# Neighborhood attention: K and V projected in halves that reach into the task loop, and an output projection issued in quarters

## The chip, the cores and the metric

The program runs on one core of one Trainium2 chip. The metric is the device time of one execution in microseconds (us), lower is better; the median of several executions is given. The engines are named as in the profile: PE is TensorE, DVE is VectorE, ACT is ScalarE, POOL is GpSimd, SP is SyncE, which issues nearly all of the DMAs.

## What is computed

The reference is two transformer layers and a third block over 256 tokens of width 1024, all in float32. Only the neighborhood attention of the second layer is touched by the change. Its input `h` is 256 x 1024; 16 heads of 64; the tokens are a grid of 4 rows and 64 columns, and a query at column c sees the 16 columns around it in all 4 rows.

```python
def _neighborhood_attention(h, w_in, w_out, rpb):
    q, k, v = jnp.split(h @ w_in, 3, axis=-1)          # w_in is 1024 x 3072
    ...
    def row_step(r):
        ...
        sc = jnp.einsum('bqhd,brqjhd->bhqrj', q_row, k_win).astype(jnp.float32) * scale
        sc = sc + bias.astype(jnp.float32)[None]
        p = jax.nn.softmax(sc.reshape(b, nh, GRID_W, kh * kw), axis=-1)
        ...
        return jnp.einsum('bhqrj,brqjhd->bqhd', p, v_win)
    o = lax.map(row_step, jnp.arange(rows))
    return o @ w_out                                    # w_out is 1024 x 1024
```

It is followed by a norm, a residual add and a feed-forward layer, called `f3` in the kernel.

## The kernel before

**Weights come in units.** A unit is 128 partitions x 2 x 512 numbers, numbered through the whole program, in a ring of RING = 6 slots. SP loads it into `raw` (`load`, L258; the two DMAs are L263), ACT rounds it into `whi` (`hi`, L265 to L272), DVE forms the rest `wlo` (`lo`, L274 to L280), and PE uses it in 12 matmuls of 512 columns, three for each pair of row block and token half (`mm3`, L282 to L289; `held_rows` and `first_chunk` do the same in another order). `hi` of unit n waits until PE has used unit n - 6; the load of unit n waits for `lo` of unit n - 6. Each engine has one instruction stream in a fixed order, and SP too: a load that waits holds up every DMA behind it.

**The projection.** `w_in` is taken in six chunks of 512 output columns, four units each: e = 0, 1 are Q, 2, 3 are K, 4, 5 are V (`chunk_pe`, L775). When a chunk is done, ACT copies token half 0 and DVE token half 1 out of PSUM into `qkv` (`evac_act` L795, `evac_dve` L802, counted in `s_qa` and `s_qv`). After chunk 4 `qk_turn` (L845) transposes Q in 16 PE instructions (L857), ACT and DVE copy it into `qB` (L1087, L1093), then, after one unit of chunk 5, it transposes K, which ACT and DVE copy into `kT` by column (L1102, L1107, four copies each, counted in `s_kta` and `s_ktv`).

**The task loop.** There are 16 tasks: a pair of heads p = 0..7 and a token half t. Task i goes through `scores(i)` on PE (L1134), bias and row maximum on DVE (L1223, L1227), two exponentials on ACT (L1208), the division on DVE (L1232, L1233), `turn(i)` on PE (L1146), a copy on ACT (L1203) and `pv(i)` on PE (L1158). PE issues per iteration: `scores(i)`, then `between(i)`, `turn(i-2)`, `pv(i-3)`. After every second task ACT and DVE split a finished head pair into `xhi` (L1184) and `xlo` (L1191), the left operand of the output projection. ACT and DVE call `between(i)` at the head of iteration i: there stand the `hi` and `lo` of coming units and the copy of chunk 5 out of PSUM.

**What PE does between the tasks** before: units 1 to 3 of chunk 5 (i = 0 to 3), and units 0 and 1 of the output projection `out1` in halves of six matmuls (i = 10, 11, 14, 15). Units 2 and 3 follow the loop; unit 4 is the first of `end_rows` (L817), then come units 5 to 7 in `held_rows` (L376 to L378).

**V by column window.** `pv` reads V from `vwin`, in the order of the column windows. `na_values_sp` (L1109, DMAs at L1117) fills it with SBUF to SBUF DMAs, 16 for each half of V, issued by SP: the first 16 after unit 6 of `out1` (wait: chunk 4 is in `qkv`), the second 16 after the load of unit j = 1 of `f3` (wait: chunk 5 is in `qkv`). `pv(0)` waits for the first 16, `pv(8)` for the second 16. Behind the second 16 SP goes on with the loads of `f3`.

Of the kernel before, what the change touches and what calls it, by code (L numbers as in the profile page):

```python
# [59 lines left out]
def build(nc, x, norm_g, ffn1_wg, ffn1_wu, ffn1_wd, ffn2_wg, ffn2_wu, ffn2_wd, diff_w_in, diff_w_out,  # L60
# [5 lines left out]
    with ctx:  # L66
# [74 lines left out]
        exw = ex[:, :, 0, :].rearrange("p b (q k) -> p b q k", q=2)  # L141
# [68 lines left out]
        s_vw = sem("window_values_landed")  # L210
# [551 lines left out]
        def proj_sp(sp, n0, w, cols=(0, 1), late=None):  # L762
            part_sp(sp, n0, w, cols)
            for j in range(UP, KT):
                down_unit(sp, n0 + j, 0, w, j * P)
                if j == 6 and late is not None:
                    late()


        def chunk_bank(e, t, m=0):  # L770
            if m == 1 and e == 5:
                return Y + 2 * t
            return (Y if e == 0 else Z + 2 * (e % 2)) + t
# [42 lines left out]

        def end_rows(pe, n0, r, nr):  # L817
# [11 lines left out]
        NEX = 3  # L829

# [11 lines left out]
        def turn_bank(kind, bk):  # L842
            return (Z + 2, Z + 3, Y + 1, Y + 3)[bk] if kind == "na" else Y + bk

        def qk_turn(pe, m, kind, which):  # L845

            for bk in range(4):
                if which == 1 and kind != "na":
                    pe.wait_ge(s_qta, 2 * m + bk + 1)
                if which == 1 and kind == "na":  # L850
                    pe.wait_ge(s_qte, 2 * bk + 2)
                    pe.wait_ge(s_qtd, 2 * bk + 2)
                for p in (2 * bk, 2 * bk + 1):
                    c0 = qk_cols(kind, p)[which]
                    for t in range(NT):
                        o = ps[:, turn_bank(kind, bk), (p % 2) * S + t * P:(p % 2) * S + (t + 1) * P]
                        ins = nc.tensor.transpose(o, qkv[:, t, c0:c0 + P], ident)  # L857
                ins.then_inc(s_qt, 1)
# [236 lines left out]
        def by_column(rows, bk):  # L1095
            return (kT[rows, 2 * bk:2 * bk + 2, :].rearrange("p a (c g) -> p a g c", g=GR),
                    ps[rows, turn_bank("na", bk)].rearrange("p (a g c) -> p a g c", a=2, g=GR))

        def na_k_act(act):
            for bk in range(4):  # L1100
# [3 lines left out]
        def na_k_dve(dve):  # L1104
            for bk in range(4):
# [12 lines left out]

        def na_pe(pe, between):
            b = NTASK  # L1120
            pe.wait_ge(s_kz, 4)
            pe.wait_ge(s_qa, 6 + 5)
            pe.wait_ge(s_qv, 6 + 5)
# [14 lines left out]
            def turn(i):  # L1138
                if i == 0:
                    pe.wait_ge(s_ktv, 8)  # L1140
                    pe.wait_ge(s_kta, 8)
                pe.wait_ge(s_a, b + i + 1)
                if i >= 2:
                    pe.wait_ge(s_ate, b + i - 1)
                for q in range(2):
                    ins = nc.tensor.transpose(ps[:, Y + 1 + 2 * (i % 2), q * P:(q + 1) * P], exw[:, i % NEX, q], ident)  # L1146
# [31 lines left out]
        def na_out_act(act, n0, p):  # L1178
            act.wait_ge(s_pv, NTASK + 2 * p + 2)
            if p == 0:  # L1180
                act.wait_ge(s_used, used(n0 + 23))
# [12 lines left out]
        def na_act(act, n0, between):  # L1194
            b = NTASK
            for i in range(NTASK + 2):
                between(i)
                if i >= 2:
                    j = i - 2
# [4 lines left out]
                if i < NTASK:  # L1204
                    p, t = TASKS[i]
                    act.wait_ge(s_mx, b + i + 1)
                    for q in range(2):
                        nc.scalar.activation(exw[:, i % NEX, q], exw[:, i % NEX, q], ACT.Exp, bias=nmx[:, i % 2, q:q + 1],  # L1208
                                             accum_out=rs[:, t, 2 * p + q:2 * p + q + 1]).then_inc(s_ex, 1)
                if i >= 5 and i % 2 == 1:  # L1210
                    na_out_act(act, n0, (i - 5) // 2)
            na_out_act(act, n0, 7)

        def na_dve(dve, steps, between):
            b = NTASK
            for i in range(NTASK + 1):
                between(i)
                if i < NTASK:
                    p, t = TASKS[i]
                    dve.wait_ge(s_sc, b + i + 1)  # L1220
                    if i >= NEX:
                        dve.wait_ge(s_at, b + i - 2)
                    steps.done(nc.vector.tensor_tensor(exw[:, i % NEX], ps[:, Z + i % 2, 0:2 * P].rearrange("p (q k) -> p q k", q=2),  # L1223
# [3 lines left out]
                    nc.vector.tensor_reduce(nmx[:, i % 2], exw[:, i % NEX], AX_X, ALU.max, negate=True).then_inc(s_mx, 1)  # L1227
                if i >= 1:
# [4 lines left out]
                    nc.vector.tensor_tensor(exw[:, j % NEX], exw[:, j % NEX],  # L1233
                                            ri[:, t, 2 * p:2 * p + 2].unsqueeze(2).broadcast_to([P, 2, P]), ALU.mult).then_inc(s_a, 1)
                if i >= 6 and i % 2 == 0:
                    na_out_dve(dve, (i - 6) // 2)
# [150 lines left out]
        def _(sp):  # L1387
# [14 lines left out]
            chunk_sp(sp, n["qkv1"], na_w_in[0], [512 * c for c in range(6)])  # L1402
# [93 lines left out]
        def _(act):  # L1496
# [22 lines left out]

            def qkv_act(m, n0, r):  # L1520
# [5 lines left out]
                if m == 1:  # L1526
                    na_q_act(act)
                    tops_act(act, n0 + UP * 5, range(1))
                    na_k_act(act)

                    def na_between(i):
                        if i == 5:
                            evac_act(act, 1, n0, 5, r, IN_ORDER)
                        if i in (1, 2, 5):
                            hi(act, n0 + UP * 5 + RING + (i + 2) // 2)
                        if i in (12, 16):
                            hi(act, n["out1"] + RING + i // 4 - 3)
                    return na_between
# [27 lines left out]
            na_act(act, n["qkv1"], qkv_act(1, n["qkv1"], 4))  # L1566
# [72 lines left out]
        def _(dve):  # L1639
# [18 lines left out]

            def qkv_dve(m, n0, r, rotate):
# [10 lines left out]
                if m == 1:  # L1670
                    na_q_dve(dve)
                    tops_dve(dve, n0 + UP * 5, range(1))
                    na_k_dve(dve)

                    def na_between(i):
                        if i == 5:
                            evac_dve(dve, 1, n0, 5, r, IN_ORDER)
                        if i in (2, 3, 6):
                            lo(dve, n0 + UP * 5 + RING + (i + 1) // 2)
                        if i in (13, 17):  # L1680
                            lo(dve, n["out1"] + RING + i // 4 - 3)
                    return na_between
# [36 lines left out]
            between = qkv_dve(1, n["qkv1"], 4, False)  # L1719
# [126 lines left out]
        def _(pe):  # L1846
# [13 lines left out]
            def qkv_pe(m, n0, r, kind):  # L1860
# [3 lines left out]
                if kind == "diff":  # L1864
                    pe.wait_ge(s_qr, 1)
                    pe.wait_ge(s_cst2, 16)
# [17 lines left out]
                def na_between(i):  # L1884
                    if i in (0, 1):
                        chunk_pe(pe, 1, n0, 5, range(i + 1, i + 2))
                    if i in (2, 3):
                        last_chunk_half(pe, n0 + UP * 5 + 3, 3, i - 2, Y, Y + 2)
# [3 lines left out]
                    if i in (10, 11, 14, 15):  # L1892
                        part_unit(pe, no, 6, i // 14, 0, (Y, Y + 2), (i % 2,))
                return na_between if m == 1 else between
# [16 lines left out]
            na_pe(pe, qkv_pe(1, n["qkv1"], 5, "na"))  # L1911
# [127 lines left out]
```

## Time and profile before

| | us |
|---|---|
| median of 3 executions | 1411.9 (1410.58 to 1412.84) |
| the profiled execution | 1412.99 |
| its span, first to last instruction | 1411.2 |
| PE busy in the span | 1387.1 |
| DVE busy | 874.5 |
| ACT busy | 752.6 |

All times in the rows are microseconds from the start of the span of that one execution. Matmuls are pipelined: a row's duration (0.39 for 512 columns) is longer than the distance to the next start (0.227), so costs on PE are taken from start to start. In the view by stretches "PEclk" is the granted TensorE clock as a share of full speed.

### The profile page before, as it was taken

Reading aid. Unit: us, or ns where it says so; the run is one execution under the profiler, and the core shown is the slowest. Engines: PE = TensorE matmul, PEld = TensorE weight load, DVE = VectorE, ACT = ScalarE, POOL = GpSimd, SP = SyncE. Lnnn points to the kernel's source line nnn. Section 1 sums busy time; section 2 is a strip of 40 time slices with the busy share of each in tenths; the row PEclk is TensorE's granted clock in tenths of the full one; section 3 lists DMA queues with packets and bytes.
Section 4 is the critical chain, followed back from the end, with each engine's and each line's share of the span. In section 5 each row is a group of like instructions: output and inputs, shape, how many; then the busy total and the mean of one; then the engine's idle time right before and its main releaser. Section 6 shows DMA issues by size and latency. Waiting matters only on the chain.

```text
span 1411.2 us, 20415 instructions
## 1 busy us (share of the span) xinstructions
PE 1387.1 (98%) x6556; PEld 1146.9 (81%) x6556; DVE 874.5 (62%) x1231; ACT 752.6 (53%) x1292; POOL 108.6 (8%) x168
## 2 busy tenths in 40 slices
PE   8999999999999999999999899999999999999999
PEld 6888878878888888888887788888888898788887
DVE  5555566777555566555666865555667876575564
ACT  6444465566444465444555765444555565565553
POOL 2322210011001000000010000000013000000000
PEclk9999999999999999999999999999999999999999
DMA  8966747315655647556555337656575523555551
GB/s 273 253 207 195 223 129 255 111 46 180 207 181 191 203 136 228 184 188 192 180 196 185 99 118 225 191 186 201 178 224 164 173 67 111 185 184 181 182 180 50
DMA packets 192565, 248.43 MB, mean 176 GB/s; under 512 B 17127, under 2 KB 130035, under 8 KB 192384
## 3 DMA queue, kind: packets, MB, share of 16 engines
q1 hardware_dynamic: 189472, 243.40, 54.8%
q0 software_dynamic: 2928, 4.31, 1.3%
q8 instruction: 30, 0.49, 0.1%
q14 instruction: 23, 0.19, 0.0%
q10 hardware_dynamic: 112, 0.05, 0.0%
HBM read 244.40 MB, written 1.18 MB: 174 GB/s over the span
## 4 chain that ended last, share of the span: by engine, by line
PE 94%; DVE 3%; ACT 2%; issue 1%; DMA 0%; ACTq 0%; DVEq 0%
PE ps L287 25%; PE ps L289 25%; PE ps L288 25%; PE ps L317 2%; PE ps L324 2%; PE ps L314 2%; PE ps L672 1%; PE ps L904 1%; PE ps L376 1%; PE ps L339 1%; PE ps L378 1%; PE ps L377 1%; ACT whi L272 1%; DVE wlo L280 1%; PE ps L1274 1%
## 5 line engine op out<-in xcount | busy, mean ns | idle before, releaser
L280 DVE TENSOR_TENSOR wlo<-raw,whi 128x1024 fp32r<-128x1024 f32 x450 | 546.6, 1226 | 351.5 <-ACT whi L272 350.9
L272 ACT CAST whi<-raw 128x1024 fp32r<-128x1024 f32 x450 | 468.9, 1051 | 324.4 <-PE ps L289 314.3
L287 PE MATMUL ps<-whi,xhi 128*128 128x512 f32 x1196 | 470.9, 394 | 0.3 <-DVE xlo L482 0.3
L289 PE MATMUL ps<-whi,xlo 128*128 128x512 f32 x1196 | 466.8, 390 | 0.0
L288 PE MATMUL ps<-wlo,xhi 128*128 128x512 f32 x1196 | 466.3, 390 | 0.0
L289 PEld LDWEIGHTS ps<-whi,xlo 128*128 128x128 f32 x1196 | 224.9, 188 | 47.3
L287 PEld LDWEIGHTS ps<-whi,xhi 128*128 128x128 f32 x1196 | 225.3, 188 | 46.3 <-issue 0.5
L288 PEld LDWEIGHTS ps<-wlo,xhi 128*128 128x128 f32 x1196 | 225.4, 188 | 45.9
L287 PE MATMUL ps<-whi,thi 128*128 128x512 f32 x384 | 153.8, 401 | 0.0
L289 PE MATMUL ps<-whi,tlo 128*128 128x512 f32 x384 | 150.2, 391 | 0.0
L288 PE MATMUL ps<-wlo,thi 128*128 128x512 f32 x384 | 149.7, 390 | 0.0
L694 ACT CAST thi<-ps 128x256 fp32r<-128x256 f32 x80 | 29.4, 373 | 106.5 <-PE ps L672 57.8
L289 PEld LDWEIGHTS ps<-whi,tlo 128*128 128x128 f32 x384 | 72.1, 188 | 15.6
L288 PEld LDWEIGHTS ps<-wlo,thi 128*128 128x128 f32 x384 | 72.3, 188 | 13.9
L287 PEld LDWEIGHTS ps<-whi,thi 128*128 128x128 f32 x384 | 72.2, 188 | 13.6
L685 ACT ACTIVATE qkv<-ps,rx 128x256 f32<-128x256 f32 x88 | 36.9, 471 | 67.8 <-PE ps L289 66.4
L720 DVE SCALAR_TENSOR_TENSOR qkv<-ps,rx,qkv 128x256 f32<-128x256 f32 x88 | 38.6, 480 | 39.2 <-ACT qkv L685 39.2
L729 DVE TENSOR_TENSOR tlo<-ps,thi 128x256 fp32r<-128x256 f32 x80 | 33.6, 424 | 41.3 <-ACT thi L694 41.3
L557 POOL TENSOR_SCALAR ry<-ssy 128x1 f32<-128x1 f32 x12 | 3.6, 300 | 592.2 <-ACT sqa L542 592.2
L317 PE MATMUL ps<-wlo,xhi 128*128 128x512 f32 x128 | 40.2, 395 | 1.7 <-DVE wlo L280 1.7
L314 PE MATMUL ps<-whi,xhi 128*128 128x512 f32 x128 | 41.1, 402 | 0.6 <-ACT whi L272 0.6
L1449 POOL DMA_DIRECT2D aux<-rpb_scratch x64 | 35.3, 559 | 75.6 <-PE ps L672 71.2
(209 smaller groups left out, 1239.0 us busy)
## 6 DMA issues: line engine op xcount, KB each, us to landing
raw<-in_ffn_wg_dram SPq DMA_DIRECT2D x176, 256.0 KB, 2.9
raw<-in_ffn_wu_dram SPq DMA_DIRECT2D x176, 256.0 KB, 3.1
raw<-in_ffn_wd_dram SPq DMA_DIRECT2D x176, 256.0 KB, 3.0
raw<-in_w_ffn_up_dram SPq DMA_DIRECT2D x88, 256.0 KB, 3.6
raw<-in_w_in_dram SPq DMA_DIRECT2D x80, 256.0 KB, 3.4
raw<-in_diff_w_in_dram SPq DMA_DIRECT2D x48, 256.0 KB, 3.2
raw<-in_na_w_in_dram SPq DMA_DIRECT2D x48, 256.0 KB, 3.2
raw<-in_w_ffn_down_dram SPq DMA_DIRECT2D x44, 256.0 KB, 3.2
```

What stands on the lines that cost most here:

```text
L272: nc.scalar.copy(whi[:, s], raw[:, s]).then_inc(s_hi, 1)
L280: nc.vector.tensor_tensor(wlo[:, s], raw[:, s], whi[:, s].bitcast(F32), ALU.subtract).then_inc(s_lo, 1)
L287: nc.tensor.matmul(outs[t], ahi[:, c], whi[:, s, i], start=start, stop=False)
L288: nc.tensor.matmul(outs[t], ahi[:, c], wlo[:, s, i], start=False, stop=False)
L289: last = nc.tensor.matmul(outs[t], alo[:, c], whi[:, s, i], start=False, stop=stop)
L314: nc.tensor.matmul(o, xhi[:, 2 * j + i, c], whi[:, s, i], start=j == 0 and i == 0, stop=False)
L317: nc.tensor.matmul(o, xhi[:, 2 * j + i, c], wlo[:, s, i], start=False, stop=False)
L685: nc.scalar.activation(silu[:, t], ps[:, base + t, 0:FC], ACT.Silu, scale=rx[:, t:t + 1]).then_inc(s_si, 1)
L694: nc.scalar.copy(thi[:, j], ps[:, Z + 2 + j, 0:S]).then_inc(s_hth, 1)
L720: nc.vector.scalar_tensor_tensor(out=hs[:, t], in0=ps[:, base + t, FC:2 * FC], scalar=rx[:, t:t + 1], in1=silu[:, t], op0=ALU.mult, op1=AL ...
L729: nc.vector.tensor_tensor(tlo[:, j], ps[:, Z + 2 + j, 0:S], thi[:, j].bitcast(F32), ALU.subtract).then_inc(s_htl, 1)
L1449: pool.dma_start(nab[cc::16, :, w], src).then_inc(s_nab, 16)
```

## The change

Q is transposed after chunk 2 and no longer after chunk 4. The order of the chunks becomes Q, Q, K first half, V first half, K second half, V second half (`NA_ORDER`). The first half of K is transposed after chunk 3; chunk 4 (K second half) has its unit 0 ahead of the loop and units 1 to 3 in iterations 0 to 2; its transposes stand in iteration 4, and in iteration 5 PE waits for all K copies. Chunk 5 runs in iterations 5 to 8, one unit each, and units 0 and 1 of `out1` in iterations 10 to 17 in quarters of three matmuls. `turn` lags `scores` by three iterations and `pv` by four; the buffers `exw` for probabilities go from 3 to 6. ACT and DVE get the same moves in their `between`. The DMAs into `vwin` are issued after unit 3 of `out1` (first half) and after unit j = 3 of `f3` (second half), and each group of 8 has a semaphore of its own. The number of matmuls, DMAs and copies is the same.

```diff
-        exw = ex[:, :, 0, :].rearrange("p b (q k) -> p b q k", q=2)
+        exw = ex[:].rearrange("p b c (q k) -> p (b c) q k", q=2)
...
         def proj_sp(sp, n0, w, cols=(0, 1), late=None):
             part_sp(sp, n0, w, cols)
+            if late is not None:
+                late()
             for j in range(UP, KT):
                 down_unit(sp, n0 + j, 0, w, j * P)
-                if j == 6 and late is not None:
-                    late()
...
+        def part_quarter(pe, n0, r, u, at):
+            pe.wait_ge(s_lo, RING + n0 + u + 1)
+            j, s, i, t = u % 2, slot(n0 + u), at // 2, at % 2
+            pe.wait_ge(s_xl, XB[r] + 2 * j + 2)
+            k, c, o = 2 * j + i, slice(t * P, (t + 1) * P), ps[:, Y + 2 * t]
+            nc.tensor.matmul(o, xhi[:, k, c], whi[:, s, i], start=k == 0, stop=False)
+            nc.tensor.matmul(o, xhi[:, k, c], wlo[:, s, i], start=False, stop=False)
+            last = nc.tensor.matmul(o, xlo[:, k, c], whi[:, s, i], start=False, stop=False)
...
+        NA_ORDER = [0, 1, 2, 4, 3, 5]
...
         def na_values_sp(sp, half):
-            sp.wait_ge(s_qa, 6 + 5 + half)
-            sp.wait_ge(s_qv, 6 + 5 + half)
+            sp.wait_ge(s_qa, 6 + 4 + 2 * half)
+            sp.wait_ge(s_qv, 6 + 4 + 2 * half)
...
-                    sp.dma_start(vwin[r::GR, w, c], qkv[p0:p0 + 32, r // 2, 2 * D + c.start:2 * D + c.stop]).then_inc(s_vw, 16)
+                    sp.dma_start(vwin[r::GR, w, c], qkv[p0:p0 + 32, r // 2, 2 * D + c.start:2 * D + c.stop]).then_inc(s_vw[2 * half + w // 2], 16)
...
-                if i in (0, 8):
-                    pe.wait_ge(s_vw, 16 * 16 * (i // 8 + 1))
+                if i % 8 < 2:
+                    pe.wait_ge(s_vw[i // 8 * 2 + i % 8], 16 * 8)
...
-            for i in range(NTASK + 3):
+            for i in range(NTASK + 4):
                 if i < NTASK:
                     scores(i)
                 between(i)
-                if 2 <= i < NTASK + 2:
-                    turn(i - 2)
-                if i >= 3:
-                    pv(i - 3)
+                if 3 <= i < NTASK + 3:
+                    turn(i - 3)
+                if i >= 4:
+                    pv(i - 4)
...
-            ffn_sp(sp, n["f3"], *ffn_w[3], 5, lambda j: na_values_sp(sp, 1) if j == 1 else None)
+            ffn_sp(sp, n["f3"], *ffn_w[3], 5, lambda j: na_values_sp(sp, 1) if j == 3 else None)
...
+            def na_qkv_dve(n0, r):
+                for e in range(4):
+                    tops_dve(dve, n0 + UP * e)
+                    evac_dve(dve, 1, n0, e, r, NA_ORDER)
+                    if e == 2:
+                        na_q_dve(dve)
+                na_k_dve(dve, range(2))
+                lo(dve, n0 + UP * 4 + RING)
+                def between(i):
+                    if i == 3:
+                        evac_dve(dve, 1, n0, 4, r, NA_ORDER)
+                    if i == 5:
+                        na_k_dve(dve, range(2, 4))
+                    if i == 9:
+                        evac_dve(dve, 1, n0, 5, r, NA_ORDER)
+                    if i in (2, 3, 4):
+                        lo(dve, n0 + UP * 4 + RING + i - 1)
+                    if i in (7, 8, 9, 10):
+                        lo(dve, n0 + UP * 5 + RING + i - 7)
+                    if i in (15, 17):
+                        lo(dve, n["out1"] + RING + i // 17)
+                return between
...
+            def na_qkv_pe(n0, r):
+                first_chunk(pe, n0, r)
+                for e in (1, 2):
+                    chunk_pe(pe, 1, n0, e, range(UP))
+                ...
+                qk_turn(pe, 1, "na", 0)
+                chunk_pe(pe, 1, n0, 3, range(UP))
+                ...
+                qk_turn(pe, 1, "na", 1, range(2))
+                chunk_pe(pe, 1, n0, 4, range(1))
+                def between(i):
+                    if i in (0, 1, 2):
+                        chunk_pe(pe, 1, n0, 4, range(i + 1, i + 2))
+                    if i == 4:
+                        pe.wait_ge(s_qa, 6 + 5)
+                        pe.wait_ge(s_qv, 6 + 5)
+                        qk_turn(pe, 1, "na", 1, range(2, 4))
+                    if i == 5:
+                        pe.wait_ge(s_kta, 8)
+                        pe.wait_ge(s_ktv, 8)
+                    if i in (5, 6, 7, 8):
+                        chunk_pe(pe, 1, n0, 5, range(i - 5, i - 4))
+                    if i == 10:
+                        pe.wait_ge(s_qa, 12)
+                        pe.wait_ge(s_qv, 12)
+                    if 10 <= i < 18:
+                        part_quarter(pe, n0 + 24, 6, (i - 10) // 4, (i - 10) % 4)
+                return between
```

ACT has the mirror of the DVE part (`na_qkv_act`): the same copies at i = 3, 5 and 9, the `hi` of units at i = 1, 2, 3, then 6 to 9, then 14 and 18.

## Rows read from the trace of the kernel before

**Rows 1.** Page: busy time, share of the span and instructions of each engine.
```profile
PE 1387.1 (98%) x6556; PEld 1146.9 (81%) x6556; DVE 874.5 (62%) x1231; ACT 752.6 (53%) x1292; POOL 108.6 (8%) x168
```

**Rows 2.** Stretches: busy PE, PEld, DVE, ACT, POOL; PEclk; DMA share; GB/s.
```profile
768.00:771.40 3.40, 3.40 (x10) 2.62 (x9) 2.30 (x4) 2.28 (x6) 0.00 (x0) 0.51 0.41 102
...
788.40:792.00 3.60, 3.44 (x17) 3.44 (x18) 3.05 (x11) 2.72 (x13) 0.00 (x0) 0.53 0.42 110
...
808.80:812.40 3.60, 3.55 (x13) 3.16 (x14) 2.45 (x5) 1.63 (x5) 0.00 (x0) 0.53 0.39 109
...
758.40:819.60 61.20, 54.02 (x302) 45.53 (x300) 45.96 (x103) 41.54 (x120) 0.00 (x0) 0.92 0.39 112
```

**Rows 3.** Waits of PE, 756 to 826: waiter, releaser, total, times, longest.
```profile
PE ps L1146 <- DVE ex L1233: 3.2, 6, 1.2
...
PE ps L1134 <- DVE kT L1107: 1.8, 1, 1.8
```

**Rows 4.** PE in time order: start, duration, line, count; idle before in brackets.
```profile
736.72 0.39 PE L287 MATMUL ps<-whi,xhi 128*128 128x512 f32 x1
...
758.48 1.91 PE L857 MATMUL ps<-cst,qkv 128*128 128x128 f32 x16
760.15 0.48 PE L287 MATMUL ps<-whi,xhi 128*128 128x512 f32 x1
...
767.14 0.68 PE L1134 MATMUL ps<-kT,qo 128*128 128x128 f32 x4 [1.82 <-DVE kT L1107]
...
772.01 0.61 PE L1134 MATMUL ps<-kT,qo 128*128 128x128 f32 x4
...
775.23 0.60 PE L1134 MATMUL ps<-kT,qo 128*128 128x128 f32 x4
...
779.77 0.61 PE L1134 MATMUL ps<-kT,qo 128*128 128x128 f32 x4
780.22 0.38 PE L1146 MATMUL ps<-cst,ex 128*128 128x128 f32 x2
780.44 0.61 PE L1158 MATMUL ps<-aT,aux 128*128 128x128 f32 x4
780.88 0.61 PE L1134 MATMUL ps<-kT,qo 128*128 128x128 f32 x4
...
796.54 0.61 PE L1158 MATMUL ps<-aT,aux 128*128 128x128 f32 x4
...
819.66 0.39 PE L376 MATMUL ps<-whi,xhi 128*128 128x512 f32 x1
```

**Rows 5.** DVE in time order: Q and K copies, a task, `lo`, copy-out, split.
```profile
761.73 2.82 DVE L1093 TENSOR_SCALAR qo<-ps 64x256 f32<-64x256 f32 x8
...
765.84 3.79 DVE L1107 COPY kT<-ps 64x512 f32<-64x512 f32 x4
...
772.66 0.42 DVE L1223 TENSOR_TENSOR ex<-ps,aux 128x256 f32<-128x256 f32 x1 [2.32 <-PE ps L1134]
...
773.99 1.22 DVE L280 TENSOR_TENSOR wlo<-raw,whi 128x1024 fp32r<-128x1024 f32 x1
...
781.74 0.75 DVE L802 TENSOR_SCALAR qkv<-ps,rx 128x512 f32<-128x512 f32 x1
...
786.21 0.85 DVE L1191 TENSOR_TENSOR xlo<-ps,xhi 64x256 fp32r<-64x256 f32 x2
```

**Rows 6.** ACT in time order: the four K copies.
```profile
764.30 3.81 ACT L1102 COPY kT<-ps 64x512 f32<-64x512 f32 x4
```

**Rows 7.** SP's queue in time order: start, time of the issues, line, count.
```profile
761.78 10.10 SPq L1117 DMA_DIRECT2D aux<-qkv  x16
...
782.81 10.23 SPq L1117 DMA_DIRECT2D aux<-qkv  x16
793.08 0.58 SPq L263 DMA_DIRECT2D raw<-in_ffn_wg_dram  x1
```

**Rows 8.** The same 32 DMAs by line: time from issue to landing.
```profile
DMA to landing us min/median/max: 2.0/2.1/2.2
```

More of the change, by code:

```diff
@@ L209, in build @@
         s_ilv = sem("rpb_interleaved")
-        s_vw = sem("window_values_landed")
+        s_vw = [sem(f"window_values_landed{i}") for i in range(4)]
         s_qtd = sem("qT_second_head_ready")
@@ L840, in keys, with turn_bank, qk_turn @@
             return t + 1 if kind == "b2" else NT
[L842 to L847, printed above, removed]
+        def turn_bank(kind, bk, which=0):
+            return (Y + 1, Y + 3, Y, Y + 2)[bk] if kind == "na" and which == 1 else Y + bk
+        def qk_turn(pe, m, kind, which, banks=range(4)):
+            for bk in banks:
                 if which == 1 and kind != "na":
                     pe.wait_ge(s_qta, 2 * m + bk + 1)
-                if which == 1 and kind == "na":
-                    pe.wait_ge(s_qte, 2 * bk + 2)
-                    pe.wait_ge(s_qtd, 2 * bk + 2)
                 for p in (2 * bk, 2 * bk + 1):
@@ L855, in qk_turn @@
                     for t in range(NT):
-                        o = ps[:, turn_bank(kind, bk), (p % 2) * S + t * P:(p % 2) * S + (t + 1) * P]
+                        o = ps[:, turn_bank(kind, bk, which), (p % 2) * S + t * P:(p % 2) * S + (t + 1) * P]
                         ins = nc.tensor.transpose(o, qkv[:, t, c0:c0 + P], ident)
@@ L1096, in by_column, with na_k_act, na_k_dve @@
             return (kT[rows, 2 * bk:2 * bk + 2, :].rearrange("p a (c g) -> p a g c", g=GR),
-                    ps[rows, turn_bank("na", bk)].rearrange("p (a g c) -> p a g c", a=2, g=GR))
-        def na_k_act(act):
-            for bk in range(4):
+                    ps[rows, turn_bank("na", bk, 1)].rearrange("p (a g c) -> p a g c", a=2, g=GR))
+        def na_k_act(act, banks):
+            for bk in banks:
                 act.wait_ge(s_qt, 8 + 4 + bk + 1)
                 nc.scalar.copy(*by_column(slice(HD, P), bk)).then_inc(s_kta, 1)
-        def na_k_dve(dve):
-            for bk in range(4):
+        def na_k_dve(dve, banks):
+            for bk in banks:
                 dve.wait_ge(s_qt, 8 + 4 + bk + 1)
@@ L1195, in na_act @@
             b = NTASK
-            for i in range(NTASK + 2):
+            for i in range(NTASK + 3):
                 between(i)
-                if i >= 2:
-                    j = i - 2
+                if i >= 3:
+                    j = i - 3
                     act.wait_ge(s_at, b + j + 1)
@@ L1207, in na_act @@
                     for q in range(2):
-                        nc.scalar.activation(exw[:, i % NEX, q], exw[:, i % NEX, q], ACT.Exp, bias=nmx[:, i % 2, q:q + 1],
+                        nc.scalar.activation(exw[:, i % NEXW, q], exw[:, i % NEXW, q], ACT.Exp, bias=nmx[:, i % 2, q:q + 1],
                                              accum_out=rs[:, t, 2 * p + q:2 * p + q + 1]).then_inc(s_ex, 1)
-                if i >= 5 and i % 2 == 1:
-                    na_out_act(act, n0, (i - 5) // 2)
+                if i >= 6 and i % 2 == 0:
+                    na_out_act(act, n0, (i - 6) // 2)
             na_out_act(act, n0, 7)
@@ L1232, in na_dve @@
                     steps.done(nc.vector.reciprocal(ri[:, t, 2 * p:2 * p + 2], rs[:, t, 2 * p:2 * p + 2]))
-                    nc.vector.tensor_tensor(exw[:, j % NEX], exw[:, j % NEX],
+                    nc.vector.tensor_tensor(exw[:, j % NEXW], exw[:, j % NEXW],
                                             ri[:, t, 2 * p:2 * p + 2].unsqueeze(2).broadcast_to([P, 2, P]), ALU.mult).then_inc(s_a, 1)
-                if i >= 6 and i % 2 == 0:
-                    na_out_dve(dve, (i - 6) // 2)
+                if i >= 7 and i % 2 == 1:
+                    na_out_dve(dve, (i - 7) // 2)
+            na_out_dve(dve, 5)
             between(NTASK + 1)
@@ L1518, in _, with na_qkv_act @@
             post_act(act, 0, 1, n["f0"] + 65, 0.5, 1, gainA(0, 2), 1)
+            def na_qkv_act(n0, r):
+                for e in range(4):
+                    tops_act(act, n0 + UP * e)
+                    evac_act(act, 1, n0, e, r, NA_ORDER)
+                    if e == 2:
+                        na_q_act(act)
+                na_k_act(act, range(2))
+                hi(act, n0 + UP * 4 + RING)
+                def between(i):
+                    if i == 3:
+                        evac_act(act, 1, n0, 4, r, NA_ORDER)
+                    if i == 5:
+                        na_k_act(act, range(2, 4))
+                    if i == 9:
+                        evac_act(act, 1, n0, 5, r, NA_ORDER)
+                    if i in (1, 2, 3):
+                        hi(act, n0 + UP * 4 + RING + i)
+                    if i in (6, 7, 8, 9):
+                        hi(act, n0 + UP * 5 + RING + i - 6)
+                    if i in (14, 18):
+                        hi(act, n["out1"] + RING + i // 18)
+                return between
             def qkv_act(m, n0, r):
@@ L1718, in _ @@
             post_dve(dve, steps, 3, n["f2"] + 65, 5, gainA(1, 2))
-            between = qkv_dve(1, n["qkv1"], 4, False)
+            between = na_qkv_dve(n["qkv1"], 4)
             dve.wait_ge(s_nar, NAP)
@@ L1863, in qkv_pe @@
                     chunk_pe(pe, m, n0, e, range(UP))
[L1864 to L1866 removed]
+                pe.wait_ge(s_qr, 1)
+                pe.wait_ge(s_cst2, 16)
                 pe.wait_ge(s_qa, 6 * m + 4)
@@ L1891, in na_between @@
                         pe.wait_ge(s_qv, 12)
-                    if i in (10, 11, 14, 15):
-                        part_unit(pe, no, 6, i // 14, 0, (Y, Y + 2), (i % 2,))
-                return na_between if m == 1 else between
+                    if 10 <= i < 18:
+                        part_quarter(pe, n0 + 24, 6, (i - 10) // 4, (i - 10) % 4)
+                return between
             def last_chunk_half(pe, n0, j, i, b0, b1):
```

73 lines of the change are left out of this document (29 added, 44 removed).

## The prediction

> **What bounds the kernel now.** The page comes first: PE is busy 98% of the span [rows 1], so the time is PE's work plus the few places where PE waits or runs slowly. In the stretches the reader looks for busy PE and granted clock together. From the end of chunk 4 (758.4) to the start of the last three projection units (819.6) PE is busy 54.0 of 61.2 us, and three spells of some 3.5 us inside it have a granted clock of 0.51 to 0.53, which is the 1.2 GHz level [rows 2]. The other stretches of the trace lose little of either kind, so this is the only place where the change can win much. The waits say who is late there: `turn` waits for DVE's division, 3.2 us in 6 places, and the first `scores` waits 1.8 us for DVE's K copies [rows 3]. DVE is busy 46.0 of the 61.2 us, ACT 41.5 [rows 2]: between the filled iterations DVE sets the pace, not PE.
>
> **Prices on PE**, start to start. 96 matmuls of 512 columns lie between 736.72 and 758.48, 0.227 each, so a unit is 2.72 and a chunk 10.9 [rows 4]. Q's 16 transposes take 1.67, half of them 0.84. An iteration with `scores` and one unit takes 3.22 (772.01 to 775.23). In a bare one `scores` is 0.45, `turn` 0.22, `pv` 0.44, together 1.11. The first `scores` and its unit took 4.87 instead of 3.22, so a slow spell costs 1.65 [rows 4].
>
> **Prices elsewhere.** DVE: a task 1.33, of which about 0.9 until the maximum; `lo` 1.2; copy-out 0.75; split 0.85; a K copy 0.95 [rows 5]. ACT's K copy is 0.95 too [rows 6]. SP: 16 value DMAs of 64 KB take 10.2 us to issue, 0.64 each, and each lands 2.1 after its issue [rows 7, 8]. One DMA of a load is 0.58, a unit has two; I take 1.0 for both [rows 7].
>
> **What is neutral.** PE gets the same matmuls and transposes. Quarters instead of halves cost some 0.09 more for each change of operand type (four more changes, 0.4, counted below). More `exw` buffers and four semaphores cost no instruction. The extra lag of one iteration gives `turn` one more iteration for the division; what it removes is the 3.2 us of rows 3, and what is late next is DVE's total work or a wait listed below.
>
> **The walk, before the loop.** The Q turn starts at 736.72, after chunk 2, and the V chunk ends at 736.72 + 1.67 + 10.97 = 749.4. Half of K's turn and unit 0 of chunk 4 end at 753.0. DVE is free 3.25 after PE ends a chunk (758.48 to 761.73), and the first `scores` came 1.30 after DVE's first K copy began (765.84 to 767.14) [rows 4, 5]: 749.4 + 4.55 = 753.9. So PE idles 0.9 here instead of 1.8.
>
> **Iterations 0 to 8.** Three iterations with a unit: 753.9 + 3 x 3.22 = 763.6. In iteration 3 DVE stands at the copy-out of chunk 4 (763.8 to 764.6), then `lo` to 765.8, then adds bias and maximum for task 3, to 766.6. PE does `scores(3)`, `turn(0)`, `scores(4)`, K's second turn (from 764.7 to 765.5), `turn(1)`, `pv(0)` and `scores(5)`, to 767.0. Then it meets the added wait for all K copies. On DVE these stand behind the rest of task 3 (0.45), a `lo` (1.2) and task 4 (1.33): 769.6, and two copies end at 771.5. PE goes on at 771.7, after some **4.7 us idle**. Queued behind that wait on PE are unit 0 of chunk 5, `turn(2)` and `pv(1)`; ACT's copy and DVE's later tasks wait for those, but have time. The restart is charged with one slow spell, 1.65, as after the 1.8 us wait of before. 771.7 + 2.8 + 0.67 + 1.65 = 776.8. Iterations 6 and 7 take 3.89 each, iteration 8 to the end of its unit 3.22. Chunk 5 is done at **787.9**, called E.
>
> **The second half of V.** What decides here is a queue. SP can issue the second 16 value DMAs only behind the load of `f3` unit 3, and that load waits for `lo` of the unit six before it, which is now DVE's `between(10)`. After E, DVE does: copy-out (E + 1.0), `lo` (2.2), task 9 (3.5), a split (4.4), `lo` (5.6). SP issues the load until 6.6, then the values: the 8th is issued at 11.1 and lands at 13.2, the 16th is issued at 16.2 and lands at **E + 18.3**. Before, the second 16 were issued from 782.81, 13.7 us ahead of `pv(8)` at 796.54, of which issue and landing need 12.3 [rows 4, 7, 8]: there was little slack. Now PE comes to `pv(8)` at about E + 9.0: it ends iteration 8 and does iteration 9 and `scores(10)` by E + 2.2, waits to 4.4 for the split that quarter 0 needs, ends iteration 10 at 5.8 (quarter 0.68, `turn` and `pv` 0.66), iteration 11 at 7.6, and stands before `pv(8)` of iteration 12 after another 1.4. `pv(8)` waits from 9.0 to 13.2, `pv(9)` after one more iteration from 15.0 to 18.3. Nothing else stands ready on PE, since its order is fixed. Loads of `f3` units 4 onward queue behind the values on SP, but PE wants them only after the whole norm and the first chunk, over 20 us later: no cost.
>
> **The end.** From `pv(9)`: 0.44, two iterations at 1.85, two without `scores` at 1.4, `turn(15)` and `pv(14)` 0.67, a wait of 0.8 for ACT (a `hi` stands before its last copy) and 0.44: 8.8. Then three units of out1, 8.2. E + 18.3 + 8.8 + 8.2 = 823.2, against 819.66 before: +3.6. A slow spell after the wait of `pv(9)` adds 1.65. **Sum: +5.3 us.** The profiled execution took 1412.99, its span 1411.2; it would become 1418.3. It lies 1.1 above the median of the runs, so for the median I say 1411.9 + 5.3 = 1417.2. The clock spells of the old stretch (three, about 5) are in its 61.2; the new walk has two in it.
>
> **The row against the page.** Rows 7 and 8 make the issue the slow part: a value DMA costs SP 0.64, 16 of them 10.2, while one lands in 2.1. The Trainium skill, DMA: Bandwidth & Descriptors, section "Issuing engines are not separate DMA queues", says that the time a sequencer needs to start a DMA is usually small beside the DMA itself. By it the 16 would land almost together; the case is priced below without the page. By that rule, the trace doesn't agree for these DMAs of 32 partitions.
>
> **Bounds of what before doesn't show.** The wait for K copies in the loop: at least 1.8, as before with the copies right behind the turn, at most 4.7 as walked; I take 4.7, since the order on DVE is fixed. Slow spells: none to four times 1.65; I take two, after the waits longer than the 1.8 that brought one before.
>
> **Rivals.**
> 1. *The values land in time* (issue cheap or overlapped, so that all 16 land about 2.1 after E + 6.6 = E + 8.7, before `pv(8)` at 9.0). Then both waits at `pv` go: E + 9.0 + 0.44 + 1.4 + 8.8 + 8.2 = E + 27.8 = 815.7, with no second spell: 4.0 before the old 819.7, **faster**, 1407.9. For it: the same DMAs held nobody before. Against it: SP's rows show 0.64 for each in both groups. It decides if the first 8 land before E + 9. Chance 0.15.
> 2. *K copies cost PE only half* (idle 2.4 and no slow spell after it), values late as forecast: 5.3 - 2.3 - 1.65 = +1.4, 1413.3, within 0.2%. For it: if DVE ran ahead of the walk in iterations 3 and 4. Chance 0.13.
> 3. *Slow spells also at the first `scores` and at the end* (before had one at each): +3.3 more, +8.6, 1420.5. For it: short waits of 0.4 to 1.0 at the end of before brought one. Chance 0.12.
> 4. *The forecast*, 1414.5 to 1420 by itself: chance 0.58. The remaining 0.02 goes to a gain of another kind, as a second cover of waits by the longer lag.
>
> **How the numbers follow.** Forecast 1417.2. The range reaches from just above rival 1, 1409.0, to rival 3 with a us for the walk, 1421.5; outside it lie about 0.15 and 0.05. 0.2% is 2.8 us, about what a measurement of this kernel can tell from no change. Slower by more: forecast and rival 3, 0.70. Within: rival 2 and a little more, 0.14. Faster: rival 1, 0.16.
>
> **What would show it.** In PE's order of time after: `scores(0)` near 753.9; a gap of 4 to 5 us before the first matmul of chunk 5 whose releaser is a K copy; E near 788; two gaps, at `pv(8)` and `pv(9)`, with a DMA into `aux` as releaser, and SP's 16 value issues beginning 6 to 7 us after E. The start of `held_rows` near 825. If `pv` shows no DMA gap the queue argument is wrong, and the result is rival 1. If the K gap is under 2.5, it is rival 2. If the division still holds `turn`, the extra lag didn't do what it says.

## The result

| | before | after |
|---|---|---|
| median, us | 1412.02 (1410.58 to 1412.84, 5 runs) | 1419.05 (1418.12 to 1421.4, 5 runs) |
| ratio to before | | 1.0053, 95% interval 1.0042 to 1.0064 |
| profiled execution, us | 1412.99 | 1421.4 |
| end of chunk 2 to the start of `held_rows`, us | 82.94 | 88.17 |

The change makes the kernel slower by 7.0 us. 1417.2 was forecast, with a range of 1409.0 to 1421.5.

The page of after: PE has 2.1 us more busy time than in [rows 1], DVE and ACT the same within 0.3, and the span is 8.4 us longer. So nearly all of it is waiting, not work. Of the 8.4 us, 5.2 lie between the end of chunk 2 and `held_rows`; the other 3.2 passed in the first 26 us of this one execution, before anything that the change touches.

```profile
span 1419.6 us, 20424 instructions
PE 1389.2 (98%) x6556; PEld 1149.0 (81%) x6556; DVE 874.7 (62%) x1231; ACT 752.4 (53%) x1292; POOL 107.9 (8%) x168
PE 94%; DVE 3%; ACT 1%; issue 1%; SPq 1%; DMA 1%; ACTq 0%; DVEq 0%
```

The last line is the chain that ended last: SP's queue and DMA have a share in it now. The waits of PE between 730 and 840 (waiter, releaser, total, times, longest):

```profile
PE ps L287 <- ACT kT L1114: 4.6, 1, 4.6
PE ps L1168 <- DMA aux<-qkv: 3.3, 1, 3.3
PE ps L1168 <- issue: 2.3, 1, 2.3
PE ps L824 <- DVE xlo L1201: 1.9, 1, 1.9
PE ps L1144 <- issue: 0.6, 1, 0.6
PE ps L1168 <- ACT aT L1213: 0.5, 1, 0.5
```

In sum these are 13.2 us. Before, PE waited 6.9 us in the same place: the 3.2 and 1.8 of [rows 3], and

```profile
PE ps L1158 <- ACT aT L1203: 1.9, 3, 1.0
```

Against [rows 3], `turn` no longer waits for the division, and the first `scores` waits 0.6 instead of 1.8. In their place PE waits 4.6 for the K copies ahead of chunk 5 (L287), 1.9 for a split ahead of quarter 0 (L824), and 2.3 and 3.3 at `pv(8)` and `pv(9)` (L1168). These are the new waits in order of time, with PE's landmarks around them:

```profile
739.88 1.91 PE L869 MATMUL ps<-cst,qkv 128*128 128x128 f32 x16
...
756.94 0.68 PE L1144 MATMUL ps<-kT,qo 128*128 128x128 f32 x4 [0.60 <-issue]
...
774.82 0.50 PE L287 MATMUL ps<-whi,xhi 128*128 128x512 f32 x1 [4.63 <-ACT kT L1114]
...
790.86 0.38 PE L1156 MATMUL ps<-cst,ex 128*128 128x128 f32 x2
...
795.17 0.47 PE L824 MATMUL ps<-whi,xhi 128*128 128x512 f32 x1 [1.93 <-DVE xlo L1201]
...
803.82 0.68 PE L1168 MATMUL ps<-aT,aux 128*128 128x128 f32 x4 [2.27 <-issue]
...
809.13 0.99 PE L1168 MATMUL ps<-aT,aux 128*128 128x128 f32 x4 [3.27 <-DMA aux<-qkv]
...
819.32 0.71 PE L1168 MATMUL ps<-aT,aux 128*128 128x128 f32 x4 [0.51 <-ACT aT L1213]
...
828.05 0.39 PE L376 MATMUL ps<-whi,xhi 128*128 128x512 f32 x1
```

The `turn` at 790.86 is the first instruction behind chunk 5: the point called E. What held the K copies is in the streams of DVE and ACT. DVE's copies (772.33) stand behind the `lo` at 769.88 and task 4, ACT's (772.82) behind the exponentials of task 4:

```profile
769.88 1.22 DVE L280 TENSOR_TENSOR wlo<-raw,whi 128x1024 fp32r<-128x1024 f32 x1
771.01 0.41 DVE L1233 TENSOR_TENSOR ex<-ps,aux 128x256 f32<-128x256 f32 x1
...
772.33 1.93 DVE L1119 COPY kT<-ps 64x512 f32<-64x512 f32 x2
...
772.82 1.95 ACT L1114 COPY kT<-ps 64x512 f32<-64x512 f32 x2
```

What held `pv` is in SP's stream. DVE ends the `lo` that starts at 795.05 at 796.28, SP issues the last load of `f3`'s first four at 796.31, and only then the 16 value DMAs:

```profile
795.05 1.23 DVE L280 TENSOR_TENSOR wlo<-raw,whi 128x1024 fp32r<-128x1024 f32 x1
...
796.31 0.37 SPq L263 DMA_DIRECT2D raw<-in_ffn_wg_dram  x1
796.72 0.47 SPq L263 DMA_DIRECT2D raw<-in_ffn_wu_dram  x1
797.29 10.23 SPq L1129 DMA_DIRECT2D aux<-qkv  x16
```

At `pv(8)` the profile names no releaser ("issue"). The eighth of the 16 is issued some 4.5 us after the first, at 801.8, and with 2.1 to land that gives 803.9, where `pv(8)` goes on at 803.82; k_gap_filled below names the DMA there.

Stretches, with the columns of [rows 2]: three slow spells again (stretches at half the clock), behind the K gap, behind the wait of quarter 0, and behind `pv(9)`.

```profile
774.60:778.00 3.40, 3.18 (x8) 2.55 (x9) 0.87 (x3) 0.17 (x1) 0.00 (x0) 0.59 0.02 6
...
795.60:799.10 3.50, 3.50 (x15) 3.08 (x14) 2.58 (x7) 2.03 (x9) 0.00 (x0) 0.51 0.54 162
...
809.10:812.70 3.60, 3.57 (x15) 3.20 (x16) 1.62 (x5) 0.00 (x0) 0.00 (x0) 0.53 0.02 5
```

### The profile page after: what moved, and what is told of

The parts are those of the page before. It is cut to its first block, busy times and chain, and to the rows that moved or that the text cites. A ratio compares the mean times of both kernels' runs of the same rounds, so it can differ in the third digit from the quotient of the medians.

```text
span 1419.6 us, 20424 instructions
## 1 busy us (share of the span) xinstructions
PE 1389.2 (98%) x6556; PEld 1149.0 (81%) x6556; DVE 874.7 (62%) x1231; ACT 752.4 (53%) x1292; POOL 107.9 (8%) x168
## 4 chain that ended last, share of the span: by engine, by line
PE 94%; DVE 3%; ACT 1%; issue 1%; SPq 1%; DMA 1%; ACTq 0%; DVEq 0%
PE ps L287 25%; PE ps L289 25%; PE ps L288 25%; PE ps L324 2%; PE ps L317 2%; PE ps L314 2%; PE ps L672 1%; PE ps L916 1%; PE ps L376 1%; PE ps L378 1%; PE ps L377 1%; PE ps L339 1%; DVE wlo L280 1%; PE ps L1285 1%; PE ps L952 1%
## 5 line engine op out<-in xcount | busy, mean ns | idle before, releaser
L287 PE MATMUL ps<-whi,xhi 128*128 128x512 f32 x1188 | 467.2, 393 | 4.9 <-ACT kT L1114 4.6
L287 PEld LDWEIGHTS ps<-whi,xhi 128*128 128x128 f32 x1188 | 223.5, 188 | 50.6 <-ACT kT L1114 4.8
L287 PE MATMUL ps<-whi,thi 128*128 128x512 f32 x384 | 153.8, 401 | 0.0
L287 PEld LDWEIGHTS ps<-whi,thi 128*128 128x128 f32 x384 | 72.2, 188 | 13.6
```

Of the source, the lines that this page charges most:

```text
L287: nc.tensor.matmul(outs[t], ahi[:, c], whi[:, s, i], start=start, stop=False)
```

## The experiments

"Stage" is the time from the end of chunk 2 to the first matmul of `held_rows`, read in one profiled execution. For kernels in the order of before, the end of chunk 2 is taken 21.76 us ahead of the end of chunk 4, as in [rows 4]. Medians of before in the three groups of runs were 1412.78, 1412.48 and 1411.86.

The mean granted clock of every one of these runs is on record too, and it tells how much of a run was spent in slow spells: one spell of 3.4 us at half the clock takes 0.0012 off the mean. The profiled executions bear this out (three spells 0.996, one 0.999, none 1.000). The 69 runs of before, by their mean clock:

| mean clock | 1.000 | 0.999 | 0.998 | 0.997 | 0.996 | 0.995 |
|---|---|---|---|---|---|---|
| runs | 8 | 8 | 18 | 7 | 19 | 9 |
| mean time, us | 1409.1 | 1410.4 | 1411.8 | 1412.0 | 1413.1 | 1414.3 |

"At equal clock" below means a comparison with this table.

### values_j1 and values_pool: who issues the second half of V, and behind what

```diff
-            ffn_sp(sp, n["f3"], *ffn_w[3], 5, lambda j: na_values_sp(sp, 1) if j == 3 else None)
+            ffn_sp(sp, n["f3"], *ffn_w[3], 5, lambda j: na_values_sp(sp, 1) if j == 1 else None)
```

> The kernel after, with one edit: the second 16 value DMAs stand behind f3's load j = 1 again, not j = 3. Theory (SP's queue sets the waits at pv(8) and pv(9)): they are issued from E + 1.0, right behind the copy-out of chunk 5, not from E + 6.5; the 8th lands at E + 7.6, before PE needs it, and the 16th at E + 12.7 instead of E + 18.3. The wait at pv(8) goes, about 2 us remain at pv(9), the stage from Q's turn to held_rows shrinks by 5.6 us, by 7.2 if the slow spell behind pv(9) goes too: median 1412 to 1413.5. Rival (DVE's work would hold PE there anyway): less than 2 us of gain, the gaps move to turn and scores.

In values_pool the call stands in POOL's stream, behind its memsets of `qB`:

```diff
-            ffn_sp(sp, n["f3"], *ffn_w[3], 5, lambda j: na_values_sp(sp, 1) if j == 3 else None)
+            ffn_sp(sp, n["f3"], *ffn_w[3], 5, None)
...
+            na_values_sp(pool, 1)
```

> The kernel after, with the second 16 value DMAs issued by POOL instead of SP. POOL has nothing else to do then and waits only for chunk 5's copy-out. Theory: issue from E + 1.0 at 0.56 each (POOL's rate for its small DMAs), the 8th lands near E + 7.3, the 16th near E + 12; SP's loads don't move. Same gain as with j = 1, 6 to 8 us. Rival (the DMAs themselves are slow, not their place in SP's queue): they land as late, measured from their first issue, as before, and PE's waits stay above 5 us in sum.

Measured: values_j1 1415.84 (ratio to before 1.0019, 1.0009 to 1.0029), stage 84.67; values_pool 1413.59 (1.0009, 0.9998 to 1.002), stage 82.43. PE and then SP of values_j1 in time order, E at 788.96:

```profile
788.96 0.38 PE L1156 MATMUL ps<-cst,ex 128*128 128x128 f32 x2
...
803.81 1.19 PE L1168 MATMUL ps<-aT,aux 128*128 128x128 f32 x4 [2.35 <-DMA aux<-qkv]
```

```profile
791.90 10.23 SPq L1129 DMA_DIRECT2D aux<-qkv  x16
```

POOL and then PE of values_pool, E at 788.41:

```profile
791.61 8.61 POOL L1129 DMA_DIRECT2D aux<-qkv  x16 [74.20 <-ACT qkv L795]
```

```profile
801.88 0.68 PE L1168 MATMUL ps<-aT,aux 128*128 128x128 f32 x4 [0.98 <-DMA aux<-qkv]
```

The place in the queue is the cause: the same DMAs, issued sooner, take away the 2.3 us at `pv(8)` and leave 2.35 (SP) and 0.98 (POOL) of the 3.27 at `pv(9)`. Both gains missed the expectation, which was 5.6 us or more: values_j1 gained 3.2 us in the median and 3.5 in the stage, values_pool 5.5 and 5.7. In values_j1 the issue began at E + 2.9, not E + 1.0: chunk 5's copy-out on ACT stands behind a copy, two exponentials and a split, and POOL names it as its releaser. So `pv(9)` went on at E + 14.9 instead of E + 18.3, which is 3.4 of the 3.5 us of the stage. The slow spell behind it came in after and in values_j1 alike. On POOL the 16 issues were also 1.6 us shorter, `pv(9)` went on at E + 13.5, and there was no spell behind it.

### k_copies_early: the K copies ahead of a `lo` and of task 4

```diff
-                    if i == 5:
+                    if i == 4:
                         na_k_dve(dve, range(2, 4))
```

and the same on ACT.

> The kernel after, with the K copies of banks 2 and 3 on ACT and DVE in between(4) instead of between(5), so ahead of one lo and of task 4's add, maximum and division. Theory (the 4.6 us gap before chunk 5's unit 0 is DVE's and ACT's order): the gap shrinks to about 2.1 us, E and everything behind it come 2.5 us sooner, 4.1 if the slow spell after the gap goes too: median 1415 to 1416.5. Rival (DVE is the bound over the stage): the work that was overtaken comes back before pv(8), gain under 1 us.

Measured: 1414.92 (1.002, 1.0009 to 1.0032), stage 84.25, 3.9 less than after. The gap is 2.19 (PE in time order), and there is no slow spell behind it (the stretch, columns as in [rows 2]):

```profile
769.04 0.50 PE L287 MATMUL ps<-whi,xhi 128*128 128x512 f32 x1 [2.19 <-ACT kT L1114]
```

```profile
769.00:773.00 4.00, 3.96 (x23) 3.37 (x23) 3.02 (x9) 1.89 (x8) 0.00 (x0) 1.00 0.55 188
```

2.4 us of gap and 1.6 of spell make up the 3.9 by which the stage is shorter, near the 4.1 expected at best. The waits behind it are the same as in after within 0.1 us, so nothing of the gain comes back, and DVE isn't the bound there.

### k_gap_filled: idle work in the gap

```diff
                     if i == 5:
+                        keep_warm(pe, 19, ps[:, Z + 3, 0:P])
                         pe.wait_ge(s_kta, 8)
```

> The kernel after, with 19 matmuls of the identity by itself (results unused, into a PSUM bank that is free) on PE right before the wait for the K copies, some 4.2 us of work in a gap of 4.6. Theory (the slow spell behind the gap comes from PE's idleness): the granted clock behind the gap stays at the full level, and the stage shrinks by the spell's 1.6 us: median 1417.4. Rival (the spell has another cause): PEclk is near 0.5 for some 3.4 us there as before, no gain.

Measured: 1418.34 (1.0044, 1.0029 to 1.0059), stage 87.24, 0.9 less than after. The clock behind the gap stays full, and E comes 49.45 us after chunk 2 instead of 50.98. The stretch behind the gap, and PE at `pv(8)`:

```profile
771.80:775.80 4.00, 3.98 (x23) 3.42 (x23) 0.70 (x3) 0.68 (x4) 0.00 (x0) 1.00 0.01 4
```

```profile
799.88 1.20 PE L1168 MATMUL ps<-aT,aux 128*128 128x128 f32 x4 [4.52 <-DMA aux<-qkv]
```

So in this execution filling the gap kept the spell away. Of the 1.5 us, 0.6 were lost again: one of SP's issues took 1.2 us instead of 0.6, the 16 took 10.86 instead of 10.23, and `pv(9)` went on at E + 18.9 instead of E + 18.3.

```profile
792.71 10.86 SPq L1129 DMA_DIRECT2D aux<-qkv  x16
```

The median gained 0.7 us, less than the 1.6 expected. The idle work does not always help: the mean clock was 0.998 in two of the eight runs, 0.996 in three and 0.995 in three, against 0.994 to 0.996 in the nine of after. At equal clock it is as slow as after.

### after_again and before_again: the same kernels once more

> The kernel after, unchanged. Its first profile has the stage from Q's turn to held_rows at 88.2 us, 5.2 more than before, but Q's turn itself 3.2 us later than before, from the first 26 us of the program, which the change doesn't touch. Theory: the stage is 88.2 us again within 0.3, and the start of Q's turn moves by some us from execution to execution without regard to the change; median 1418 to 1419.5. Rival (the change also slows the start): Q's turn at 739.5 to 740 again.

> The kernel before, unchanged, to see its own stage again. Its first profile had three slow spells in the stage and took 82.9 us from the end of chunk 2 to held_rows; before_j3, the same order of work plus a wait of 2.0 us, had none and took 81.3. Theory: the waits of PE are the same in every execution (6.9 us), and the number of slow spells is not: 0 to 3, each 1.6 us, so the stage is 78.0 to 82.9 us and the time differs by as much. Then part of after's loss in the medians beyond the stage's 5.2 us is that its longer waits bring spells every time. Rival (spells are fixed): three spells at the same places, stage 82.9.

Measured: after_again 1419.09 (1.0046, 1.003 to 1.0063), stage 88.57 (0.1 more than expected at most), and it begins at 736.95, as before's at 736.72: the 3.2 us of the first profile were of that execution's first 26 us and not of the change. before_again 1411.01 (1.0003, 0.9993 to 1.0013), stage 80.5, with one slow spell, not three (0 to 3 were expected); the waits of [rows 3] are the same to 0.1 us, and one of 0.4 for a split is new. Its whole stage, and its waits of PE:

```profile
736.60:817.20 80.60, 73.01 (x398) 60.69 (x397) 56.97 (x113) 51.00 (x130) 0.00 (x0) 0.98 0.47 144
```

```profile
PE ps L1146 <- DVE ex L1233: 3.2, 6, 1.2
...
PE ps L1134 <- DVE kT L1107: 1.8, 1, 1.8
```

So the waits of one kernel hardly change from execution to execution, and the number of its slow spells does. After's stage was 5.2 and 5.6 us above before's first one, but 7.6 and 8.0 above its second. The medians' 6.6 to 7.0 lie between. The clocks on record say why: all nine runs of after are at 0.994 to 0.996, while most of before's are higher. At equal clock after is 4.7 us slower at 0.995 (seven runs, mean 1419.0) and 5.0 at 0.996 (one run), which is the stage's difference; the rest of the medians' difference is that before often has fewer spells.

### before_j3: the later place in SP's queue alone

```diff
-            ffn_sp(sp, n["f3"], *ffn_w[3], 5, lambda j: na_values_sp(sp, 1) if j == 1 else None)
+            ffn_sp(sp, n["f3"], *ffn_w[3], 5, lambda j: na_values_sp(sp, 1) if j == 3 else None)
```

> The kernel before, with one edit: the second 16 value DMAs stand behind f3's load j = 3 as in the kernel after, not j = 1. Theory (SP's queue): they are issued from about 786.0 instead of 782.8, behind the lo of unit out1 + 5 (783.75 to 785.0) and one load; the last lands near 797.7, so pv(8) waits about 1 us where it had none, and the stage grows from 82.9 to 84 to 85.5: median 1 to 2.5 us above before's. Rival: SP has slack enough, no change.

Measured: 1412.6 (1.0003, 0.9994 to 1.0013). The wait at `pv(8)` is there, 2.0 us and not the 1 expected, but the median, which should have risen by 1 to 2.5 us, didn't move: the number of spells changes it by as much. At equal clock the ten runs are 1.2 us slower on average. The profiled execution had no spell in a stage of 81.2, where before_again with one took 80.5. PE at `pv(8)`, and the stage with its full clock:

```profile
796.27 0.68 PE L1158 MATMUL ps<-aT,aux 128*128 128x128 f32 x4 [2.04 <-issue]
```

```profile
736.60:817.80 81.20, 71.55 (x397) 59.47 (x396) 57.03 (x113) 51.03 (x130) 0.00 (x0) 1.00 0.46 143
```

The later place alone costs before about 1 us; together with the rest of the change it costs 5.5 us of waiting, since there DVE reaches that `lo` only in iteration 10.

### before_lag: the longer lag alone

```diff
+        NEXW = 6
...
-                if 2 <= i < NTASK + 2:
-                    turn(i - 2)
-                if i >= 3:
-                    pv(i - 3)
+                if 3 <= i < NTASK + 3:
+                    turn(i - 3)
+                if i >= 4:
+                    pv(i - 4)
```

with ACT, DVE and the splits of head pairs moved to match, and a semaphore for each half of V.

> The kernel before with one part of the change alone: turn lags scores by three iterations, pv by four, six exw buffers (and a semaphore for each half of V, which that order needs). Theory (DVE's total work sets the pace in the bare iterations 4 to 9, the lag only moves its waits): the waits of turn for the division, 3.2 us in 6 places, shrink below 1 us, but waits of scores or pv for DVE come in their place, and the stage without spells shrinks by 1 us or less; median within 0.1% of before. Rival (latency of the chain scores, maximum, exponential, division is what turn waits for): the stage shrinks by 3 to 5 us, median 1408 to 1410.

Measured: 1412.84 (1.0007, 0.9998 to 1.0017), stage 84.3 with three spells, against 82.9 with three. PE's waits from 736 to 820:

```profile
PE ps L1159 <- DVE xlo L1192: 2.4, 2, 1.7
PE ps L287 <- DVE xlo L1192: 2.3, 2, 2.1
PE ps L1159 <- ACT aT L1204: 2.2, 3, 1.2
PE ps L1135 <- DVE kT L1108: 1.8, 1, 1.8
```

The waits for the division (L1146 of before) are gone, and 4.7 us for the splits, which the lag makes an iteration later too, stand in their place. As expected, other waits came in place of those that went: 8.7 us in sum instead of 6.9. The lag alone gains nothing; at equal clock its ten runs are 1.1 to 2.0 us slower.

### k_early_split, chunk5_sooner and quarters_later: the waits taken away together

k_early_split is k_copies_early, with the second half of V issued half by SP (behind j = 1) and half by POOL:

```diff
+            ffn_sp(sp, n["f3"], *ffn_w[3], 5, lambda j: na_values_sp(sp, 1, range(2)) if j == 1 else None)
...
+            na_values_sp(pool, 1, range(2, 4))
```

> The kernel after with two edits: K copies in between(4), and the second half of V issued half by SP (behind f3's load j = 1) and half by POOL. Theory: both waits at pv are gone, the K gap is 2.2 us without a slow spell behind it; one spell is left, behind the wait of quarter 0 for the split, and it now costs its 1.6 us. Stage 77 to 79 us against before's 82.9: median 1407.5 to 1409.5, faster than before. Rival (without the waits DVE becomes the bound: it is busy 57 us of the stage in both kernels, in bursts): new waits of turn for the division appear, stage 80 to 83.

chunk5_sooner also takes the wait for the K copies from chunk 5 to `pv(0)`, moves the second half of K into other PSUM banks for that, and makes the splits of head pairs and ACT's and DVE's moves for the units earlier:

```diff
-            return (Y + 1, Y + 3, Y, Y + 2)[bk] if kind == "na" and which == 1 else Y + bk
+            return (Y + 1, Y + 3, Z + 2, Z + 3)[bk] if kind == "na" and which == 1 else Y + bk
...
-                    if i == 5:
-                        pe.wait_ge(s_kta, 8)
-                        pe.wait_ge(s_ktv, 8)
-                    if i in (5, 6, 7, 8):
-                        chunk_pe(pe, 1, n0, 5, range(i - 5, i - 4))
+                    if i in (4, 5, 6, 7):
+                        chunk_pe(pe, 1, n0, 5, range(i - 4, i - 3))
...
-                    if 10 <= i < 18:
-                        part_quarter(pe, n0 + 24, 6, (i - 10) // 4, (i - 10) % 4)
+                    if 9 <= i < 17:
+                        part_quarter(pe, n0 + 24, 6, (i - 9) // 4, (i - 9) % 4)
```

> The kernel after rearranged: second half of K transposed into the banks of pv, so that chunk 5 starts in iteration 4 (units in 4 to 7) and only pv(0) waits for the K copies; K copies in between(4); quarters in iterations 9 to 16; the splits of a head pair one step earlier on ACT and DVE; V's second half issued half by SP, half by POOL. Theory (the loss of the kernel after is its three waits and their spells, not the longer filled loop): the K gap is under 1 us, quarter 0 doesn't wait, no wait at pv(8) or pv(9); stage 74 to 77 us against 82.9 of before, median 1404.5 to 1407.5. Rival (DVE-bound loop): stage over 79, with turn waiting for DVE in several iterations.

quarters_later is chunk5_sooner with the quarters back in iterations 10 to 17:

> chunk5_sooner with the quarters of the output projection in iterations 10 to 17 instead of 9 to 16, since quarter 0 still waited 2.4 us for the split of head pair 1 on DVE. Theory: scores, turn and pv of iterations 9 and 10 run in that time, the wait shrinks below 1 us, the stage from 74.9 to 73.5 to 74.5 us, median 1404 to 1405.5. Rival (DVE is behind anyway and the wait moves to turn or to scores): stage 74.9 within 0.4.

Measured: k_early_split 1408.29 (0.9976, 0.9966 to 0.9986), stage 78.0; **chunk5_sooner 1405.68 (0.9956, 0.9942 to 0.997), stage 74.9**; quarters_later 1405.93 (0.9964, 0.9951 to 0.9976), stage 75.7. chunk5_sooner's waits of PE and its whole stage:

```profile
PE ps L824 <- DVE xlo L1204: 3.2, 2, 2.4
PE ps L1171 <- ACT aT L1218: 0.9, 2, 0.6
PE ps L1171 <- DVE kT L1119: 0.8, 1, 0.8
PE ps L1144 <- issue: 0.6, 1, 0.6
```

```profile
736.70:811.60 74.90, 69.41 (x398) 59.14 (x397) 56.99 (x113) 50.81 (x130) 4.36 (x8) 1.00 0.50 155
```

k_early_split came out as expected: no wait for values, a K gap of 2.2 without a spell, one spell behind quarter 0, and no new wait above 0.6. In chunk5_sooner the wait for K is 0.8 and there is none at `pv(8)` or `pv(9)`, and what is in the main the order of work of after beats before by 6 to 7 us. At equal clock it is 3.5 us (mean clock 1.000, 1405.6 against 1409.1); the rest is that PE's clock stayed full, as in three of its five runs. Quarter 0's wait for its split stayed, 2.4 us, against the expectation. Moving the quarters later didn't help: the wait became one of `pv` for ACT's copy (3.4 us in 4 places), so the expectation of quarters_later fell. Its rival was right that DVE is late anyway, but the stage, 0.8 longer, lies outside its bounds too. DVE is busy 57 us of the 75 in chunk5_sooner; that its bursts are what is left was not tested.

## Why the prediction was right

Every landmark, after minus the 3.16 us of later start:

| step of the prediction | forecast | measured |
|---|---|---|
| first `scores` | 753.9, idle 0.9 | 753.8, idle 0.6 |
| gap for the K copies | 4.7 | 4.63 |
| E | 787.9 | 787.7 |
| quarter 0 goes on | E + 4.4 | E + 4.3 |
| values issued from | E + 6.6 | E + 6.4 |
| PE stands before `pv(8)` | E + 9.0 | E + 10.7 |
| `pv(8)` goes on | E + 13.2 | E + 13.0 |
| `pv(9)` goes on | E + 18.3 | E + 18.3 |
| wait at the end for ACT | 0.8 | 0.5 |
| stage against before | +5.3 | +5.2 |

- **The queue argument** (SP behind a load, the load behind DVE's `between(10)`) held, and values_j1 and values_pool show it as the cause. Its rival, values in time, fell: the wait is there. Issuing the 16 took 10.23 us on SP and 8.61 on POOL, with 2.1 and 2.3 from issue to landing. The Trainium skill, DMA: Bandwidth & Descriptors, section "Issuing engines are not separate DMA queues", calls the time to issue a DMA usually small beside the DMA itself. Here it was 0.64 beside 2.1, and five times the landing for the 16 in a row; the measurement decides.
- **The K gap** held, and k_copies_early shows its cause, the order on DVE and ACT.
- **Slow spells**: two exposed ones were charged, after the K gap and after `pv(9)`, and both came. A third, behind quarter 0's wait, was not forecast. It brought PE to `pv(8)` 1.7 us late, so that it waited 2.3 there and not the 4.2 of the walk, and cost nothing. k_gap_filled, whose profile has no spell there, shows the walk as forecast: PE stands before `pv(8)` at E + 9.1 and waits 4.5. The reason given, that a wait longer than 1.8 us brings a spell, was wrong: a gap of 2.19 brought none in k_copies_early, 1.8 none in before_j3. And the prediction did not follow it, since its own walk had four such waits (4.7, 2.2, 4.2 and 3.3) and it charged two. That two was the right number is in part luck.
- **The size in the medians**, 7.0 instead of 5.3: the term that was missing is before's own variation. The sum took its three spells as given, while many runs of before have fewer, as their clocks show, and all of after's are at 0.994 to 0.996. At equal clock the difference is 4.7 to 5.0.
- **The bound for chunk 5's copy-out** used DVE's time (E + 1.0). ACT's is E + 2.9. That was hidden behind the `lo` of after, and made the expectation of values_j1 too high.
- **The lag**: the prediction said DVE's work or a listed wait would be next. before_lag shows it: 3.2 us for the division became 4.7 for splits.

## What to carry to other kernels

When work moves in a loop, follow what else is queued on its completion: here a DMA group behind one more load meant behind a `lo` two iterations later, and PE waited 5.5 us although no instruction was added. Filling the loop with more matmuls is worth it only if the waits placed between them are for something that the other engines did first; the same order with the K copies first and V's DMAs spread over two queues turned +0.5% into -0.4%. Where runs of one kernel differ by slow clock spells, compare stages spell by spell or runs of equal mean clock, and don't read 2 us in a median.

## What the runs showed of the hardware

- The granted TensorE clock fell to half (1.2 GHz) for some 3.4 us at a time after idle gaps, but the same gap did not always bring it. Before had three such spells in the stage in one execution and one in another, though the gaps ahead of them (1.8, 1.2 and 1.0 us) were there both times and equal to 0.1 us; before_j3 had the gap of 1.8 and no spell.
- 4.4 us of idle matmuls in a 4.6 us gap kept the clock full behind it in the profiled execution. after_again had the clock low from 769 to 776, through the gap itself.
- The mean granted clock of a run accounts for most of the scatter of before: 1409.1 us at 1.000, 1414.3 at 0.995, by estimate some 1.3 us for each spell (5.2 us over 0.005 of clock, 0.0012 for a spell).
- POOL issued a 64 KB DMA in 0.54 us, SP in 0.64, and the 16 landed 2.3 and 2.1 us (median) after issue: POOL was the faster to issue and a little slower to land.
- The start of the program (first loads, in after's first profile a slow spell from 14 to 21 us) moved everything behind it by up to 3.2 us between executions.
